# An output projection done as seven block products over token and head halves, with its weight sums made on GpSimd during the banded attention

## What is computed

```python
h = rms_norm(x, norm_mix_pre)
z = h @ w_in                                  # 1024 x 2816
a = window_attention(rope(aq), rope(ak), av, attn_sink)   # 8 heads of 64, window 128
a = rms_norm(a, attn_out_norm)                # 1024 x 512
r = retention(rq, rk, rv, rg, decays, ret_gn) # 4 heads of 128, two directions
mix = concatenate([a, r], -1) @ w_out         # (1024 x 1024) @ (1024 x 1024)
x = x + rms_norm(mix, norm_mix_post)
h = rms_norm(x, norm_xa_pre)
mn = rms_norm(mem, norm_mem)                  # 256 memory tokens
kv = mn @ xa_wkv                              # keys and values, 1024 x 2048 weights
```

## Time and profile before

| | |
|---|---|
| median of 3 runs | 1403.66 us (1403.32 to 1403.76) |
| the profiled execution, its own time | 1403.7 us |
| its span in the profile | 1401.9 us |
| PE busy | 1382.9 us, 6756 matmuls and transposes recorded |
| DVE, POOL, ACT busy | 859.3, 821.1, 646.3 us |
| share of PE in the chain that ended last | 85% |

### The profile page before, as it was taken

One profiled execution on the slowest core, in us unless ns is written; L12 is line 12 of the kernel. 1 busy time (PEld: TensorE's weight loads), 2 busy tenths in 40 slices (PEclk: granted clock), 3 DMA queues, 4 the chain that ended last, 5 costly groups with the idle time before them and its releaser, 6 DMA issues.

```text
span 1401.9 us, 18901 instructions
## 1 busy us (share of the span) xinstructions
PE 1382.9 (99%) x6756; PEld 1151.7 (82%) x6756; DVE 859.3 (61%) x1264; ACT 646.3 (46%) x1315; POOL 821.1 (59%) x574
## 2 busy tenths in 40 slices
PE   7999999999999999999999999999999999999998
PEld 7998888767988888888888888888888888878886
DVE  5799996887855768764267543333323333484868
ACT  6432233677554854354375533333333333544454
POOL 1697266103582665611354687787777774799653
PEclk9999999999999999999999999999999999999999
DMA  5676133200043464311535132333333324933353
GB/s 202 212 247 206 46 95 101 61 1 2 1 151 125 135 229 134 96 34 31 187 107 201 53 113 98 113 113 112 99 105 98 113 84 167 365 105 98 111 206 150
DMA packets 127309, 172.04 MB, mean 123 GB/s; under 512 B 9584, under 2 KB 73456, under 8 KB 127216
## 3 DMA queue, kind: packets, MB, share of 16 engines
q1 hardware_dynamic: 123776, 161.52, 35.3%
q10 hardware_dynamic: 3440, 9.32, 1.9%
HBM read 129.64 MB, written 41.16 MB: 122 GB/s over the span
## 4 chain that ended last, share of the span: by engine, by line
PE 85%; POOL 5%; DVE 5%; ACT 2%; issue 2%; DMA 2%; SPq 0%; DVEq 0%; POOLq 0%; ACTq 0%
PE ps L1167 25%; PE ps L1169 25%; PE ps L1168 25%; PE ps L1163 5%; PE ps L1598 2%; PE ps L1341 1%; PE ps L1455 1%; POOL wd L1133 1%; PE ps L1379 1%; DMA gain_b<-f_rows 1%; POOL w_lo L1051 1%; PE ps L1433 1%; POOL right_b L1124 1%; DVE x L3360 1%; POOL right_a L1124 1%
## 5 line engine op out<-in xcount | busy, mean ns | idle before, releaser
L1167 PE MATMUL ps<-w_hi,t_hi 128*128 128x512 f32 (+2 forms) x592 | 225.6, 381 | 1.7 <-DVE t_lo L2616 1.3
L1169 PE MATMUL ps<-w_hi,t_lo 128*128 128x512 f32 (+2 forms) x592 | 223.9, 378 | 0.0
L1168 PE MATMUL ps<-w_lo,t_hi 128*128 128x512 f32 (+2 forms) x592 | 223.8, 378 | 0.0
L962 POOL TENSOR_TENSOR w_lo<-raw,w_hi 128x512 fp32r<-128x512 f32 (+1 forms) x52 | 82.0, 1584 | 96.5 <-ACT w_hi L1877 96.4
L1167 PEld LDWEIGHTS ps<-w_hi,t_hi 128*128 128x128 f32 x592 | 111.2, 188 | 20.6 <-DVE t_lo L2616 1.7
L1169 PEld LDWEIGHTS ps<-w_hi,t_lo 128*128 128x128 f32 x592 | 111.2, 188 | 18.4
L1168 PEld LDWEIGHTS ps<-w_lo,t_hi 128*128 128x128 f32 x592 | 111.2, 188 | 17.8
L3253 DVE TENSOR_TENSOR ev<-ps,ev 128x512 f32<-128x512 f32 x21 | 14.5, 692 | 138.6 <-PE ps L1169 138.6
L1051 POOL TENSOR_TENSOR w_lo<-raw,w_hi 128x512 fp32r<-128x512 f32 x32 | 41.8, 1315 | 98.4 <-ACT w_hi L2264 98.2
L2463 ACT ACTIVATE ev<-ps 128x512 f32<-128x512 f32 x63 | 37.5, 595 | 83.8 <-PE ps L1169 83.8
L1877 ACT ACTIVATE w_hi<-raw 128x512 fp32r<-128x512 f32 (+1 forms) x52 | 31.4, 616 | 96.5 <-PE ps L1169 96.1
(11 more groups left out here) (374 smaller groups left out, 4037.2 us busy)
## 6 DMA issues: line engine op xcount, KB each, us to landing
raw_a<-in_ffn_w_gu_dram SPq DMA_DIRECT2D x44, 256.0 KB, 3.2
raw_b<-in_ffn_w_gu_dram SPq DMA_DIRECT2D x44, 256.0 KB, 3.2
f_rows<-fs SPq DMA_DIRECT2D x44, 256.0 KB, 3.7
gain_b<-f_rows SPq DMA_DIRECT2D x39, 256.0 KB, 2.7
tables<-f_rows SPq DMA_DIRECT2D x38, 256.0 KB, 2.7
f_rows<-fa SPq DMA_DIRECT2D x33, 256.0 KB, 3.5
raw<-in_xa_wkv_dram SPq DMA_DIRECT2D x32, 256.0 KB, 3.4
raw<-in_xa_wo_dram SPq DMA_DIRECT2D x32, 256.0 KB, 2.6
```

The source lines that it names most:

```text
L962: nc.gpsimd.tensor_tensor(w_lo[:, k, 0:width], raw[:, k, 0:width], w_hi[:, k, 0:width].bitcast(F32), ALU.subtract).then_inc(w_split, 1)
L1167: nc.tensor.matmul(out, a_hi, b_hi, start=start, stop=False, skip_group_check=onto)
L1168: nc.tensor.matmul(out, a_hi, b_lo, start=False, stop=False, skip_group_check=onto)
L1169: return nc.tensor.matmul(out, a_lo, b_hi, start=False, stop=stop, skip_group_check=onto)
```

## The change

The tokens are halved (tiles 0 to 3, 4 to 7), the inner dimension is halved into attention and retention, and the output columns too. Seven products of 4 weight units by 4 tiles take the place of eight. Four of them need sums of weight quarters, and three sums of token quarters.

- *Weight sums.* For each of four slices SP loads the four quarters (128 x 512 each) into the free query columns of z, POOL makes four sums, SP stores them to `o_sums` in device memory. This stands between the loading of the first four weights and the retention. ACT waits for the stores before it writes into these columns.
- *Products.* In this order: 11, S1, S4, S2, S3, 22, 12. S4 accumulates onto the banks of S1, S3 and 22 onto those of S2. ACT keeps the results of 11 and S1 in `part`, DVE joins the others into y. The attention rows are turned as tiles 4 to 7 ahead of product 11 and as differences of tiles (made by POOL) within it; the retention rows within S1 and within S4.
- *Sums of tokens.* ACT copies turned rows unrounded into z, DVE and POOL make the three sums, and ACT and DVE split them.
- *Weights.* All but the first four of the 28 units are rounded by ACT and split by POOL.
- *Order.* The attention rows are normed in the order 4, 5, 6, 0, 7, 1, 2, 3; ACT norms all four heads of tiles 6 and 7; the x tiles are loaded back by SP between weights instead of by ACT at once; the memory rows lie in z and are turned behind S3.

```diff
+PRODUCTS_O = ("11", "S1", "S4", "S2", "S3", "22", "12")
+NORM_ORDER = (4, 5, 6, 0, 7, 1, 2, 3)
+ALL_HEADS_ON_ACT = (6, 7)
...
             out_loads(0, RING)
...
-            out_loads(RING, 2 * NK)
+            o_sums_load(0)
+            o_sums_load(1)
+            for r in range(RING):
+                o_sums_store(r)
+                if r + 2 < RING:
+                    o_sums_load(r + 2)
...
+            out_loads(RING, 17)
+            sp.wait_ge(turned, TURNED["mem"])
+            x_back(0, 3, 5)
+            out_loads(17, 20)
+            sp.wait_ge(o_low, O_LOW + 4)
+            x_back(1, 2, 4)
+            out_loads(20, 24)
...
+            def o_sums_load(r):
+
+                if r == 0:
+                    sp.wait_ge(turned, TURNED["qk"] + 18)
+                if r >= 2:
+                    sp.wait_ge(o_out[r % 2], O_OUT + 64 * (r // 2))
...
             for k in range(RING):
                 split(U_O, U_O, k, 512)
+            for r in range(RING):
+                a11, a12, a21, a22 = (o_stage(r, b) for b in range(4))
+                pool.wait_ge(o_in[r % 2], O_IN + 64 * (r // 2 + 1))
+                nc.gpsimd.tensor_tensor(a21, a21, a22, ALU.add).then_inc(o_summed, 1)
+                pool.wait_ge(o_summed, O_SUMMED + 4 * r + 1)
+                nc.gpsimd.tensor_tensor(a11, a21, a11, ALU.subtract).then_inc(o_summed, 1)
+                pool.wait_ge(o_summed, O_SUMMED + 4 * r + 2)
+                nc.gpsimd.tensor_tensor(a12, a12, a11, ALU.subtract).then_inc(o_summed, 1)
+                nc.gpsimd.tensor_tensor(a22, a22, a11, ALU.subtract).then_inc(o_summed, 1)
...
+            for m in range(4):
+                pool.wait_ge(a_n, max(normed_rows(m), normed_rows(4 + m)))
+                v = z[:, m, C_Q:C_K]
+                nc.gpsimd.tensor_tensor(v, v, z[:, 4 + m, C_Q:C_K], ALU.subtract).then_inc(o_diff, 1)
...
+            def o_free(kind, m):
+
+                lows = DVE_EV["c"] + m + 1
+                if kind == "11":
+                    pe.wait_ge(dve_ev, lows)
...
+                elif kind == "S4":
+                    pe.wait_ge(part_out, 4 + m + 1)
+                    pe.wait_ge(dve_ev, lows + 8)
+                elif kind == "S2":
+                    pe.wait_ge(dve_ev, lows + 12)
+                    pe.wait_ge(o_t4, O_T4 + m + 1)
...
+            def o_product(j, behind=lambda k: None):
+
+                kind = PRODUCTS_O[j]
+                first = kind in ("11", "S1", "S2")
+                for k in range(RING):
+                    pe.wait_ge(w_split, U_O + RING * j + k + 1)
...
+            o_product(0, turn_differences)
+            o_product(1, turn_first_rows)
+            o_product(2, turn_second_rows)
+            o_product(3)
+            o_product(4)
...
+            o_product(5)
+            last_product()
...
             post_rows(1)
+            mem_low(1)
             dve.wait_ge(gb_in, 64)
             pre_rows(0)
             post_rows(2)
+            for m in range(4):
+                o_join(5, m)
             pre_rows(1)
+            o_join(6, 0)
+            o_join(6, 1)
             post_rows(3)
-            mem_low(0)
+            o_join(6, 2)
+            post_rows(4)
             pre_rows(2)
-            mem_low(1)
+            o_join(6, 3)
+            post_rows(5)
+            pre_rows(3)
+            post_rows(6)
+            pre_rows(4)
+            post_rows(7)
```

More of the change, by code:

```diff
@@ L165, in kv_beside, with normed_rows @@
     return NK + RING <= n < 2 * NK
+def normed_rows(t):
+    return NORM_ORDER.index(t) + 1
 def qk_bank(i):
@@ new lines, in o_part @@
+            def o_part(kind, k, m, first, final, onto=False):
+                kk, c0 = o_slots[kind]
+                c = slice(c0 + m * P, c0 + (m + 1) * P)
+                return three(ps[:, o_bank0(kind) + m, :], t_hi[:, kk + k, c], t_lo[:, kk + k, c],
+                             w_hi[:, k, :], w_lo[:, k, :], first, final, onto)
+            def o_product(j, behind=lambda k: None):
[3 more added lines that the diff above has]
+                    pe.wait_ge(w_split, U_O + RING * j + k + 1)
+                    if kind in ("S2", "S3", "22") and k % 2 == 0:
+                        pe.wait_ge(o_low, O_LOW + 2 * ("S2", "S3", "22").index(kind) + k // 2 + 1)
+                    for m in range(4):
+                        if k == 0:
+                            o_free(kind, m)
+                        last = o_part(kind, k, m, first and k == 0, k == RING - 1, not first)
+                        if m == 3:
@@ L1472, in half_product, with last_product @@
                             last.then_inc(w_used, 1)
-                        elif k == k0 + 3:
+                        elif k == RING - 1:
                             last.then_inc(tile_done, 1)
+                    behind(k)
+            def last_product():
+                for m in range(4):
+                    o_free("12", m)
+                    for k in range(RING):
+                        if m == 0:
+                            pe.wait_ge(w_split, U_O + 6 * RING + k + 1)
+                        last = o_part("12", k, m, k == 0, k == RING - 1)
+                        if m == 3:
+                            last.then_inc(w_used, 1)
+                        elif k == RING - 1:
+                            last.then_inc(tile_done, 1)
@@ new lines, in turn_differences, with turn_first_rows @@
+            def turn_differences(k):
+                if k == 1:
+                    for m in range(4):
+                        pe.wait_ge(o_diff, O_DIFF + m + 1)
+                        pe.wait_ge(o_raw, O_RAW + m + 1)
+                        turn_half(m, m, C_Q)
+            def turn_first_rows(k):
+                if k == 2:
+                    for m in range(4):
+                        pe.wait_ge(mixed, m + 1)
+                        pe.wait_ge(part_out, m + 1)
+                        turn_half(4 + m, m, C_RQ)
@@ L1476, in _, with turn_second_rows @@
+            def turn_second_rows(k):
+                if k == 1:
+                    for m in range(4):
+                        pe.wait_ge(mixed, 4 + m + 1)
+                        pe.wait_ge(o_t2, O_T2 + m + 1)
+                        turn_half(4 + m, 4 + m, C_RQ)
             chunk_products(0)
@@ L2921, in _ @@
                     statistics(done)
-            for t in range(NT):
-                lo_half(t, 0)
+            for n in range(4):
+                o_rows_low(n)
             statistics(RH - 1)
@@ L2929, in _ @@
                                            op1=ALU.mult).then_inc(r_n, 1)
+            for n in range(4, 8):
+                o_rows_low(n)
             for t in range(NT):
+                if t in ALL_HEADS_ON_ACT:
+                    continue
                 for h in range(2):
```

406 lines of the change are left out of this document (275 added, 131 removed).

## The result

The changed kernel takes **1409.88 us** (median of four runs, 1407.63 to 1413.46) against 1403.68 of the kernel before in the same job: ratio 1.0046, 95% interval 1.0033 to 1.0058. It is slower, where 1402.3 us was forecast, and it lies outside the range of 1397.0 to 1406.0. The profiled execution is the one of 1407.63 us.

The account below looks back on a forecast made before the run. PE was taken as the bound, busy 1382.9 of 1401.9 us. From 1403.7, minus 10.9 for removed matmuls, plus 5.2 for new waits and 4.3 in the attention, came 1402.3 us; 8-in-10 range 1397.0 to 1406.0.

Parts of the forecast that it names:

- Removed, 10.9 us: Output projection: 48 fewer matmuls at 0.2268 us each take 10.9 us off PE, all on the path.
- Waits in the projection, 4.6 of the 5.2: New PE waits within the projection; with 0.6 us behind it, the new waits sum to 5.2 us.
- First rows: Projection start: PE, free after only 16 transposes, waits 0.35 us for the first operand's low part.
- S1: Second product of the projection: PE waits 1.4 and 1.1 us for POOL's low parts behind mixed rows, together 2.5.
- S1 into S4: Projection: S4 waits 1.45 us for ACT's copies of S1's banks, queued behind a weight rounding.
- the last product: Projection's last product: its fourth weight's low part comes late, about 0.3 us.
- Attention, 4.3 us: Banded attention: VectorE's tiny operations wait out POOL's weight sums, costing 4.3 us, from 0 to 12.6.
- Rivals A and B: A: attention untouched, 1398.0 us, chance 0.22. B: everything hidden, no new wait, 1392.8 us, chance 0.06.
- Behind the projection, 0.6 us with ends at 0 and 3.5: After the projection: VectorE's extra joins and row make PE wait for freed banks, 0.6 us, 0 to 3.5.
- Rival C: Attention: each round of POOL's sums meets an odd step, losing 12.6 us, 1410.6; with two rounds, 1406.1; chance 0.10.
- what would show the forecast wrong: Tiny operations at 0.16 us beside POOL, no PE wait in S1, or PE waiting over 3 us at rows behind the projection.

Follow-up runs that it names:

- b1: Changed kernel with two orders turned in the projection: POOL's low parts ahead of mixes, ScalarE's copies of S1's banks ahead of roundings; 1406.3 us.
- a0: Changed kernel with the 16 weight sums of the attention made on one column of each block instead of 256; 1405.4 us.
- a1: Changed kernel with all 16 weight sums made, each pair begun only after VectorE's small operations of a step; 1405.3 us.
- c1: Changed kernel with ScalarE's roundings of the memory's key weights moved ahead of the sums of squares that wait for VectorE's joins; 1411.5 us.
- c4: Changed kernel with the memory's second product's eight low parts on VectorE instead of POOL, roundings and first row blocks' low parts moved ahead; 1406.4 us.
- the second job: The job that ran the changed kernel again, without edit, as yardstick for the follow-ups: 1408.0 us, ratio 1.003 to the kernel before.
- d3: d2 with one more wait: POOL begins the third token sum only after VectorE's two low parts of the first sum; 1400.1 us.
- d4: d1 with one more wait: POOL begins the third token sum only after VectorE's two low parts of the first sum; 1400.0 us.
- d2: d1 with the eight low parts of the memory's second product made by VectorE instead of POOL; 1400.8 us.
- d1: Changed kernel with a1, b1 and c1 together, and VectorE's low parts of the first two row blocks ahead of the last row block's result; 1400.0 us.

## Why the prediction was wrong

**Removed, 10.9 us: right.** 48 matmuls are gone. From B to C the time fell by 5.5, so 5.4 us of it went into waits.

**Waits in the projection, 4.6 of the 5.2: right, a little small.** First rows 0.7 (381.55 + 1.71 to 383.93) for 0.35; S1 2.5 for 2.5 by b1; S1 into S4 1.5 for 1.45; the last product 0.4 for 0.3. The places and the engines were those named.

**Attention, 4.3 us: the mechanism right, the price of a step too high.** 2.3 and 2.7 us in the changed kernel, 2.3 to 5.0 over seven profiles. That the tiny operations wait for POOL is what a0 and a1 show, and POOL's rounds came where they were forecast. But "each tiny operation waits out a POOL operation: 0.65 us on average for the first, 1.25 for each one behind it" priced a step at 1.9 or 3.15 us. In the profile of the changed kernel only one operation of a step waited, for 1.03 to 1.25 us; two full waits in one step are seen in c1 and c4 (5.0 and 4.7 us lost). So a loss near 4.3 was within reach of the spread, and the changed kernel itself lay below it. The Trainium skill, SBUF — State Buffer, section Who interferes with whom, has a VectorE instruction with two SBUF inputs contend with a GpSimd instruction that reads SBUF. The trace agrees: an operation of 0.16 us takes up to 1.25. Rivals A and B fell; C was not reached in the attention.

**Behind the projection, 0.6 us with ends at 0 and 3.5: here it failed.** It measured 7.3. The step said of VectorE: from "42.4 us, 6 idle, I get 43 busy", so its first low parts come at 489 to 490, PE is late by 0.6. Two things were wrong. First, durations were taken as they were before, when VectorE and POOL worked apart more often; with the gaps filled, 12 of 21 row operations take 2.1 us or more, from 474.91 on all but one. 450.26 to 498.80 is 48.5 us without a gap, not 43: the 20 operations of before are 3.3 us longer in sum, and most of the rest is the one more row, whose two operations take 2.11 and 1.65 us where 1.8 was counted for both. I had weighed the blocking for the attention and did not apply it here. Second, I asked only which bank VectorE frees for PE, and not who else it slows: POOL's low parts, at 2.17 us a weight that feeds PE 1.36. PE first stopped for POOL at 489.48. That is 486.1 on the clock of the prediction (the projection began 3.4 us later here), 5 us before the 491.0 at which it was to stop for VectorE. At the turned rows themselves it waited only 0.3 us (499.11 + 0.23 to 499.62). With 7.3 in place of 0.6, 0.8 more in the projection and 2.7 in place of 4.3, the sum gives 1408.2, and the second job measured 1408.0; the 0.6 us that came back elsewhere are in neither and stay unexplained.

Rival C, the slower side, had 0.10 and the wrong place. The statement of what would show the forecast wrong had the right stretch ("PE waiting at the turned rows behind the projection by more than 3 us"), but with VectorE as the bound and not POOL, and without a price or a chance of its own.

## What to carry to other kernels

Before giving POOL or VectorE more work with two SBUF inputs, list where the other has such work in the same stretch, and cost each at the other's operation on top of its own. Idle time of either is then not free: it is what keeps the two apart. Where they must meet, order them by a semaphore, so that POOL starts behind VectorE's short operations and leaves a gap where VectorE has something urgent. That cost nothing here, and none of the twelve runs of d3 and d4 fell into the second group of times.

## What the runs showed of the hardware

- The wait doesn't depend on the size of the waiting operation, and goes both ways: one column on VectorE 1.13 us instead of 0.16, one column on POOL 1.18 instead of 0.19. Where both have an operation ready they mostly alternate: POOL's take 2.17 us each and VectorE's 2.1 to 2.2, where they take 1.3 alone.
- An operation of VectorE can wait through several of POOL that begin after it: 7.2 us through four, with a gap of 0.17 us as its end. The Trainium skill, SBUF — State Buffer, section Who interferes with whom, has the one that issues first hold the ports for its whole instruction while the other blocks; that alone doesn't tell this, and the trace does. Whether it gets in between two of them differs from run to run, and fits the two groups of times, 5 to 6 us apart.
- Waits of PE in a stage that it used to fill can cost clock as well: 0.78 over the 6 us in which a wait of 2.35 us lies (b1), 0.72 over the 6 us from shortly before the end of a wait of 2.24 (c1) and of one of 4.37 (d2). The waits of 0.6 us in the changed kernel left it at 1.00, and so did one of 1.95 us (d1 and d4).
